# Early transposes, earlier weight splits and a shorter path to the routing picks in an encoder block with a mixture of experts

## What is computed

```
xn = rmsnorm(h, norm_mix_g)
zu, zv, q, k, va, ga, gb = split(xn @ w_in)
y_a = (gelu(zu) * (W_s @ layernorm(gelu(zv)) + b_s)) @ w_branch_a
y_b = sliding_window_attention(q, k, va, sinks) @ w_branch_b
h = h + (sigmoid(ga) * y_a + sigmoid(gb) * y_b) @ w_out
hn = rmsnorm(h, norm_ffn_g)
gsel = argmax(hn @ w_rg + b_rg)              # best group of four
topv, topi = top_k(elog of that group, 2)    # two experts of eight
tw = softmax(topv) * softmax(glog)[gsel]
h = h + sum over the two experts: tw * (silu(hn @ w_gate) * (hn @ w_up)) @ w_down
out = rmsnorm(h, norm_final_g)
```

## Time and profile before

| What | Before |
|---|---|
| Median of 3 runs | 910.32 us (909.59 to 910.58) |
| The profiled execution | 909.68 us |
| Its span in the trace | 907.9 us |
| TensorE busy | 856.5 us, 94% |
| VectorE busy | 426.2 us, 47% |
| ScalarE busy | 216.2 us, 24% |
| DMA | 246.86 MB, mean 272 GB/s |

### The profile page before, as it was taken

One profiled execution on the slowest core, in us unless ns is written; L12 is line 12 of the kernel. 1 busy time (PEld: TensorE's weight loads), 2 busy tenths in 40 slices (PEclk: granted clock), 3 DMA queues, 4 the chain that ended last, 5 costly groups with the idle time before them and its releaser, 6 DMA issues.

```text
span 907.9 us, 11349 instructions
## 1 busy us (share of the span) xinstructions
PE 856.5 (94%) x4631; PEld 553.3 (61%) x4631; DVE 426.2 (47%) x811; ACT 216.2 (24%) x397; POOL 3.7 (0%) x17
## 2 busy tenths in 40 slices
PE   8999999999999999999999985999996799999986
PEld 7888888777777888888734442453641353644532
DVE  5538325677674344436787122434332214435123
ACT  6422222464444222223211110100110001100114
POOL 0000000000000100000000000000000000000000
PEclk9999999999999999999999997999997899999998
DMA  8554212122222743692589999999999999999994
GB/s 291 143 98 115 97 47 93 47 93 69 72 93 66 222 115 93 266 403 75 204 320 428 417 427 427 427 427 427 429 426 430 428 427 427 427 430 426 426 412 188
DMA packets 68839, 246.86 MB, mean 272 GB/s; under 512 B 22536, under 2 KB 46128, under 8 KB 55216
## 3 DMA queue, kind: packets, MB, share of 16 engines
q1 hardware_dynamic: 68704, 246.07, 69.3%
q10 hardware_dynamic: 80, 0.02, 0.0%
HBM read 243.98 MB, written 2.10 MB: 271 GB/s over the span
## 4 chain that ended last, share of the span: by engine, by line
PE 83%; DMA 9%; DVE 4%; issue 2%; ACT 2%; SPq 0%; DVEq 0%; ACTq 0%
PE bank L904 18%; PE bank L591 9%; PE bank L593 9%; PE bank L592 9%; PE bank L961 8%; DMA R<-w_down 5%; DMA R<-w_up 3%; PE bank L618 2%; PE bank L619 2%; PE bank L620 2%; PE bank L870 2%; PE by_side L870 2%; PE bank L989 2%; PE bank L948 2%; PE bank L990 1%
## 5 line engine op out<-in xcount | busy, mean ns | idle before, releaser
L904 PE MATMUL bank<-R,packT 128*64 128x512 f32 (+1 forms) x1004 | 187.7, 611 | 20.1 <-DMA R<-w_up 10.6
L904 PEld LDWEIGHTS bank<-R,packT 128*64 128x64 f32 (+1 forms) x1004 | 58.7, 129 | 131.1 <-issue 130.6
L1438 DVE TENSOR_TENSOR wlo<-raw,whi 128x2048 fp32r<-128x2048 f32 x33 | 75.5, 2287 | 84.8 <-ACT whi L1139 84.7
L591 PE MATMUL bank<-xnT_hi,whi 128*128 128x512 f32 x288 | 113.6, 395 | 1.8 <-DVE wlo L1438 1.8
L593 PE MATMUL bank<-xnT_hi,wlo 128*128 128x512 f32 x288 | 112.2, 389 | 0.0
L592 PE MATMUL bank<-xnT_lo,whi 128*128 128x512 f32 x288 | 112.1, 389 | 0.0
L961 PE MATMUL bank<-R,actT 128*64 128x512 f32 (+1 forms) x384 | 73.8, 628 | 7.5 <-DMA R<-w_down 7.2
L1139 ACT ACTIVATE whi<-raw 128x2048 fp32r<-128x2048 f32 x33 | 63.0, 1908 | 67.7 <-PE by_side L593 33.8
L1920 DVE SCALAR_TENSOR_TENSOR y_lo<-bank,small,y_hi 128x512 fp32r<-128x512 f32 x26 | 19.4, 751 | 91.1 <-ACT y_hi L1338 91.1
L591 PEld LDWEIGHTS bank<-xnT_hi,whi 128*128 128x128 f32 x288 | 54.1, 188 | 13.3 <-issue 2.5
L593 PEld LDWEIGHTS bank<-xnT_hi,wlo 128*128 128x128 f32 x288 | 54.1, 188 | 11.5
(11 more groups left out here) (388 smaller groups left out, 1305.9 us busy)
## 6 DMA issues: line engine op xcount, KB each, us to landing
R<-w_up SPq DMA_DIRECT2D x28, 2048.0 KB, 18.4
R<-w_gate SPq DMA_DIRECT2D x26, 2048.0 KB, 19.7
R<-w_down SPq DMA_DIRECT2D x23, 2048.0 KB, 19.6
raw<-w_in SPq DMA_DIRECT2D x17, 1024.0 KB, 5.1
R<-w_down SPq DMA_DIRECT2D x10, 1024.0 KB, 10.0
R<-w_gate SPq DMA_DIRECT2D x8, 1024.0 KB, 9.9
R<-w_up SPq DMA_DIRECT2D x7, 1024.0 KB, 11.1
raw<-w_in SPq DMA_DIRECT2D x20, 256.0 KB, 4.5
```

Of the source, the lines that this page charges most:

```text
L591: pe.matmul(dst, hi_w, hi_x, start=start, stop=False)
L904: mm = pe.matmul(dst[s * w:(s + 1) * w, :], packT[:, c, odd * P + s * w:odd * P + (s + 1) * w], part_of(s, c) if part_of else R[2 * slots[ ...
L1438: dve.tensor_tensor(wlo[c % 2][:, :], raw[c % 2][:, :], whi[c % 2][:, :].bitcast(F32), ALU.subtract).then_inc(lo_split, 1)
```

## The change

Three edits, with no work added or taken away.

- TensorE turns the upper channel blocks 4 and 5 right behind `turn_x(1)`, ahead of the wait for the second pair's copied rows, instead of behind channel blocks 0 and 1 of the second pair. Blocks 6 and 7 stay.
- ScalarE splits unit 14 behind the Gelu of tile g = 5 and ahead of slot 0 (before: behind slot 0), and unit 15 behind the Gelu of tile g = 7 and ahead of slot 2 (before: behind slot 2). VectorE splits unit 14 behind slot 0, at the head of g = 6 (before: behind slot 1, at the head of g = 7), and unit 15 ahead of slot 3 (before: behind slot 3).
- VectorE's subtractions for `gexp` and `gap` move behind `picked`, `sel_a` and `sel_b`.

```diff
                 for pair in range(2):
                     if pair == 1:
                         turn_x(1)
+                        turn_upper(0)
+                        turn_upper(1)
...
-                        for t in range(TT):
-                            mm = pe.transpose(bank[4 + k][:, t * P:(t + 1) * P], xn_tok[:, t, (WIDE + k) * P:(WIDE + k + 1) * P],
-                                              ident[:, :])
-                        mm.then_inc(xnT_psum, 1)
+                        if k >= 2:
+                            turn_upper(k)
...
             for c in range(ZU, GA):
-                start_unit(c)
+                if c < GA - 1:
+                    start_unit(c)
                 for m in range(2):
                     g = 2 * (c - ZU) + m
                     gate_tile(20 + g, ACT.Gelu)
+                    if g in (5, 7):
+                        start_unit(GA - 1 if g == 5 else GA)
                     if g >= 5:
                         attention_slot(g - 5)
             for u in range(4):
-                start_unit(GA + 2 * u)
+                if u:
+                    start_unit(GA + 2 * u)
...
-                    if m == 1:
+                    if m == (0 if c == GA - 1 else 1):
                         start_unit(c)
...
             for u in range(4):
+                if u == 0:
+                    start_unit(GA)
                 for m in range(2):
                     attention_slot(3 + 4 * u + m)
-                    if m == 0:
+                    if m == 0 and u:
                         start_unit(GA + 2 * u)
...
-            dve.tensor_tensor(gexp[:, :, :], glog, wide_t(gmax, NG), ALU.subtract).then_inc(route_sub, 1)
...
-            dve.tensor_tensor(gap, v2, v1, ALU.subtract).then_inc(route_sub, 1)
...
             in_all_groups(sel_b, second_8).then_inc(choices_spread, 1)
+            dve.tensor_tensor(gexp[:, :, :], glog, wide_t(gmax, NG), ALU.subtract).then_inc(route_sub, 1)
+            dve.tensor_tensor(gap, v2, v1, ALU.subtract).then_inc(route_sub, 1)
```

More of the change, by code:

```diff
@@ L630, in first_unit, with turn_upper @@
                 pe.wait_ge(vecs_ready, 1)
+                def turn_upper(k):
+                    for t in range(TT):
+                        mm = pe.transpose(bank[4 + k][:, t * P:(t + 1) * P], xn_tok[:, t, (WIDE + k) * P:(WIDE + k + 1) * P],
+                                          ident[:, :])
+                    mm.then_inc(xnT_psum, 1)
                 for pair in range(2):
```

## The result

| | Before | After |
|---|---|---|
| Median of 6 runs | 910.45 us (909.27 to 911.28) | 904.86 us (904.38 to 905.93) |
| Ratio | | 0.9943, 95% interval 0.993 to 0.9956 |
| The profiled execution, its span | 909.68 us, 907.9 us | 905.82 us, 904.0 us |

The change makes the kernel 5.2 us faster by the ratio, in the interval from 4.0 to 6.4 us; the two medians are 5.6 us apart. The direction was right, the size was not: 3.5 us were forecast.

What follows compares the result with a forecast made beforehand. TensorE bounds the kernel up to 425 us, the DMA stream from 470 to 885 us, but its loads wait for TensorE. Savings of 0.87 + 2.45 + 0.18 = 3.50 us gave 906.8 us, range 905.3 to 908.8 us.

Steps and rivals of the forecast that it cites:

- Edit A: First unit, TensorE: eight transposes moved into the wait before 19.00 us cost nothing there; 0.87 us saved, at least 0.71.
- The extra 0.16 us for two changeovers: First unit: the first matmul behind transposes takes longer than the others; two fewer such changeovers may save 0.16 us.
- Edit B: Units 14 and 15 split earlier on ScalarE and VectorE: 1.90 us plus 0.55 us, together 2.45 us saved.
- late next: Slot 3, waiting for VectorE's read of slot 2's scores, limits unit 14's gain: 1.90 of 1.97 us hold.
- ScalarE's cover of 1.12 us: Unit 14's moved high split is hidden before slot 0's first Exp, which waits for VectorE, with 1.12 us to spare.
- The 2.5 us for unit 14's load: Unit 14's 1 MB load, issued 13.9 us before its moved high split, takes 2.5 us at 426 GB/s.
- the 1.38 us of drain: The skill's drain behind ScalarE's table load would cost edit B 0.26 us; the sum went by the rows, without it.
- Edit C: Routing, VectorE: two subtractions moved off the way to the picks, 0.18 us saved, between 0 and 0.34 us.
- The expert half moves as a whole: Every microsecond saved before 442 us counts in full; the rival that the expert half takes it back: 910.3 us, chance 0.06.
- The sum, 3.50 us: Whole kernel: 0.87 + 2.45 + 0.18 us saved, giving 906.8 us; 2.92 us with lower bounds.
- a rival, with a chance of 0.11: First gather, 445 to 448 us: the clock may no longer fall to 0.50, saving 1.2 us more, 905.6 us; chance 0.11.
- The signs of being wrong: A wait before slot 3, matmuls resuming later than 19.1 us, or a different count of 1.2 GHz matmuls in the gather.

Runs made afterwards that it cites:

- both first profiles: The first profiled executions of the kernel before and of the kernel with all three edits: 909.68 us and 905.82 us.
- The second profile of the kernel before: The kernel before run once more, unchanged, against itself as a control: 909.42 us against 909.82 us, ratio 1.0001.
- the third of the changed kernel: Profile of the kernel with all three edits, timed a third time against the kernel before: 905.73 us against 909.23 us, ratio 0.9958.

## Why the prediction was wrong, step by step

**Edit A, 0.87 us: right.** 15.01 to 14.13 us from the first product to unit 1, and 0.87 us less in the first stretch with A alone (185.69 to 184.82). The extra 0.16 us for two changeovers was real.

**Edit B, 2.45 us: right.** 2.34 us alone, and 3.29 us together with A where the sum says 3.32. The wait that was to be "late next", at slot 3, is there with 0.19 us, and taking VectorE's side alone showed that it costs 2.24 us when ScalarE's round isn't shortened too. ScalarE's cover of 1.12 us measured 1.21 us. The 2.5 us for unit 14's load were too short: in the trace of before it landed 6.1 us behind its issue, still well inside the 13.9 us. On the rule of the Trainium skill (ScalarE: Activation LUTs, What ACT_TABLE_LOAD costs) the trace again disagrees: a function follows the load by 0.01 us, so the 1.38 us of drain isn't paid here.

**Edit C, 0.18 us: right.** 0.14 to 0.16 us in the second stretch with C alone, and 0.17 us in the chain itself with all edits, too small for the runs to show.

**The expert half moves as a whole: right.** 454.1 us from the first gate product to the end in both first profiles.

**The sum, 3.50 us: right where the clock is the same.** The second profile of the kernel before and the third of the changed kernel both have no low clock near the routing. From the first product to the first gate product they take 441.05 us (11.25 to 452.30) and 437.53 us (11.43 to 448.96), 3.52 us less.

**The step that failed is the clock.** The prediction took the fall in the gather as a property of the kernel before and kept it in its main case on both sides, so that its term in the sum was nothing; only a rival, with a chance of 0.11, let it go. But the profile of before was one draw: in the second profile of the same kernel the fall isn't there. In the pair of first profiles it lay in the gather before and ahead of the ranks after. That made the third stretch 0.88 us shorter (11.79 to 10.91) and took 0.12 us of edit C's 0.17 us back in the second, 0.76 us in all, where the sum had nothing. From the first product to the first gate product it is 442.49 us before and 438.28 us after, 4.21 us less. The rival had the fall in the gather at 1.2 us; it measures 1.48 us. Its 905.6 us came nearest to the 904.86 us. The Trainium skill (TensorE: Matmul & The Clock Gate, Part 1: The HAM clock gate) says that the number of matmuls at the low clock differs between runs of one kernel. It says so of a kernel's start; here the trace agrees in the middle of one, with 16 matmuls in 3 us at a clock of 0.50 in one profile and 27 at 1.00 in the other. I had quoted it and not used it.

**The base and the scatter were mis-sized too.** The forecast started from 910.32 us, the median of three runs, where 79 runs have a mean of 909.59 us and a standard deviation of 0.98 us. The range allowed 0.3 us for scatter. Over all runs the change is worth 4.22 us, so some 1.0 of the 5.2 us is the chance of six runs on each side: 910.45 and 904.86 us both lean outward from 909.59 and 905.37 us. The mean of the 22 runs lies just inside the range, so that the median of six lies outside it is in part bad luck.

**The signs of being wrong.** Of the three that the prediction named two are there: a wait in front of slot 3 (0.19 us, small) and another count of matmuls at 1.2 GHz in the gather. The third isn't: the matmuls resume at 19.36 us, but that is 7.69 us behind the first product, as before.

**What stays open** is why the low clock is rarer with the change. If each run were a draw of its own, 1 or none of 22 in the first row, with 26 of all 101 there, would have a chance under 0.01, so luck alone is unlikely but not excluded. Single edits had mean clocks of 0.9802 (A), 0.9808 (B), 0.9805 (C) and 0.9808 (A and B) in 5 to 12 runs each, too few to say which edit does it. How often the fall lands in the gather, in the warm-keeping products or nowhere isn't known either: there are two profiles of the kernel before and four of the changed kernel.

## What to carry to other kernels

A wait for a weight split was cured mostly by taking a split out of the round of another engine (ScalarE's Gelu, gating, slot, Exp), and moving only VectorE's splits, which TensorE waited for, made the kernel slower. Where edits are worth a few microseconds, cut the trace at events of the program and compare stretches: these agreed with the sum to 0.1 us, while whole executions of one kernel scatter by 4 us (907.84 to 911.99). A low clock seen in one profile can be a draw, as it was here; profile the same kernel twice before it goes into a base or a sum.

## What the hardware showed unexpectedly

The clock fell to 0.50 not only behind gaps. In the kernel after it fell just before 434 us, and TensorE was busy in all of the 3.00 us before 434 and in all of the 4.00 us behind it. Just before stood transposes and the router's products of 36 columns:

```profile
...
429.58 1.07 PE L789 MATMUL bank<-ident,h_tok 128*128 128x128 f32 x8
430.49 1.87 PE L801 MATMUL bank<-w_router,hgT 128*128 128x36 f32 x16
432.19 2.07 PE L801 MATMUL by_side<-w_router,hgT 128*128 128x36 f32 x16
...
```

Whether it is these that let it fall was not tested; the same products stand in the profiles without a fall. And with the warm-keeping products removed altogether, 5.17 us of idle time before the ranks, the gather lost only some 0.5 us and the kernel 0.2 to 0.9 us.
